# First recurrence of a two-block network: from head pairs one after another to time quarters with all pairs at once

## The chip, the cores and the metric

The kernel runs on one core of a Trainium2 chip. The metric is the device time of one execution in microseconds. It is built as a sequence of blocks of engine programs; between two blocks all engines meet.

## The reference, cut to what matters

The program is two network blocks on 1024 tokens of width 1024. The change is in the first block's recurrence. There are 8 heads of 64 channels; per head a 64x64 state S goes through all tokens:

```
wf = decay_w0 + tanh(wd) @ decay_up;  decay = exp(-exp(-softplus(-wf) - 0.5))
a  = sigmoid(iclr_a0 + ad @ iclr_up);  g = sigmoid(gd) @ gate_up
kk = (k * k_k) normalised per head;    k = k * (1 + (a - 1) * k_a)
S_t = S_{t-1} * decay_t + (S_{t-1} @ -kk_t) (kk_t * a_t)^T + v_t k_t^T
y_t = S_t @ r_t
rwkv_out = (head_group_norm(y) * lnx_g + lnx_b + sum(r * k * r_k) * v) * g
```

Everything is float32. Before this stage a projection has written r, k and v as feature rows, and the low-rank inputs; after it a convolution branch is normalised and both go through an output projection, a feed-forward part, and then the second block.

## The kernel before, in words

All line numbers are those of the profile. `recurrence1` (L513 to L914) holds five engine programs that run beside each other, each in its own order, tied by semaphores. The tokens are cut into 16 chunks of 64. A pair is two heads, one on partitions 0 to 63 and one on 64 to 127. Each engine has one loop over the four pairs, `with pe.Fori(0, PAIRS) as j` on TensorE; the order inside it is written out by hand. Every product is named (`act_names`, `dve_names`, `pe_names`, `pool_names`), the class `Made` counts them on one semaphore per engine, and `need(...)` on TensorE waits for a name. One pass of the loop, for one pair and all its 16 chunks, has these stages:

1. Preparation. TensorE makes the low-rank products `decay` and `iclr` (`broad`, L776, 512 columns each), ScalarE their sigmoids (L639, L641). VectorE scans the logarithms of decay along each chunk (L692) and ScalarE makes three exponentials (L645 to L647). Sums of squares per head go through `stats` (L787), a square root, a reciprocal, a copy to full width and `scales` (L793). VectorE makes the six scaled operands (L709 to L720), each 128x1024.
2. Chunk scores and transposes. `turn` (L825) transposes v, b and k by products with the identity; `LB` and `LK` (L838) are the chunk scores, masked by VectorE (L725).
3. Inverses. For each chunk and head a 64x64 triangular matrix is inverted in 6 levels, in two batches of 8 chunks. GpSimd masks the matrix for a level (L627). TensorE makes T = L X (L782), ScalarE copies it out (L659), TensorE makes two products from it, for X and for its transpose, and VectorE adds them (L739, L740). Level 0 has a product with a unit matrix as well, for the transpose (L734).
4. Chunk walk. For each chunk `ch` in turn: G on TensorE (L874, L875), a copy by ScalarE (L663), U (L782), a copy by VectorE (L743), the state products S (L885, L886), and the new state by VectorE (L748) from those and from the old state scaled by ScalarE (L666). The outputs Y (L892 to L894) are issued after S. All tiles are 64x64 for two heads, and the copies 128x64.
5. Results. Mean, variance, normalisation, the bonus term and the gate (L753 to L768, L776, L787, L793), each 128x1024.

The next pair's stage 1 begins when the results of this one are on their way. The constants (masks) are loaded by the sync engine at the start (L604) and the slices of the low-rank weights in the loop (L611).

Of the kernel before, what the change touches and what calls it, by code (L numbers as in the profile page):

```python
# [14 lines left out]
ALU = mybir.AluOpType  # L15
ACT = mybir.ActivationFunctionType
# [4 lines left out]
P = 128  # L21
T = 1024
# [46 lines left out]
def shape_constants():  # L69
# [15 lines left out]
    out["tile_run"] = np.broadcast_to((np.arange(T2) % P != 0).astype(float), (P, T2))  # L85
    windows = np.array([2, 4, 8, 16])[:, None]
# [422 lines left out]
BATCH = 8  # L509
LEVELS = 6  # L510

def recurrence1(nc, ins, consts, table, ident, rkv, low):  # L513
# [9 lines left out]
    act_names = (["sg", "a", "square", "p", "pinv", "pprev", "kk_std", "v"]  # L523
                 + [f"{x}t{b}" for x in "vbk" for b in range(2)]
                 + [f"T{l}{b}" for l in range(1, LEVELS) for b in range(2)]
                 + [x for ch in range(NC1) for x in ((f"G{ch}", f"SP{ch}") if ch else (f"G{ch}",))]
                 + ["y", "y_square", "y_std"])
    dve_names = ["kkr", "sg_sum", "before_sum", "kk_floor", "kat", "kf", "bon", "kk_inv",
                 "kk_wide"]
    dve_names += ["kk", "at", "rt", "b1", "bt", "kt"]  # L530
    for q in range(4):
        dve_names += [f"LB{q}", f"LK{q}"]
    for b in range(2):
        dve_names += [f"XT0{b}"]
    for b in range(2):
        dve_names += [f"X0{b}"]
    for l in range(1, LEVELS):
        for b in range(2):
            dve_names += ([f"X{l}{b}"] if l < LEVELS - 1 else []) + [f"XT{l}{b}"]
    for ch in range(NC1):  # L540
        dve_names += [f"U{ch}", f"S{ch}"]
    dve_names += ["yc", "y_inv", "y_wide", "yn", "ynorm", "bonus", "ysum", "gated"]
    pe_names = ["decay", "iclr", "kk_stats", "kk_scale"]
    pe_names += ["vt0", "vt1"]
    for q in range(4):
        pe_names += [f"LB{q}", f"LK{q}"]
    pe_names += ["bt0", "bt1", "kt0", "kt1", "T00", "T01"]
    for l in range(1, LEVELS):
        for b in range(2):
            pe_names += [f"T{l}{b}"]  # L550
        for b in range(2):
            pe_names += [f"X{l}{b}"]
    for ch in range(NC1):
        pe_names += [f"G{ch}", f"U{ch}", f"S{ch}", f"Y{ch}"]
    pe_names += ["mean", "y_stats", "y_scale", "bonus", "gate"]
    pool_names = [f"LM{l}{b}" for l in range(LEVELS) for b in range(2)]

    with Scope(nc, "rec1") as s:
        masks = {}
        for name in ("head_ones", "head_sel", "before", "upto", "levels", "eye", "chunk_run"):  # L560
            masks[name] = s.sb(name, [P, CONST_AT[name][1]])
        both = s.sb("both", [P, 2, C1])
        ups = s.sb("ups", [P, 3, P])
        cols = s.sb("cols", [P, 4])
        gn_eps = s.sb("gn_eps", [P, 1])

        def wide(name):
            return s.sb(name, [P, T])

        sg, a, p, pinv, kkr, kk, kf, bon, sq, cumt = map(  # L570
            wide, ("sg", "a", "p", "pinv", "kkr", "kk", "kf", "bon", "sq", "cumt"))
        ar = s.sb("ar", [P, NC1, 2, C1])
        b_, k_, v_ = map(wide, ("b", "k", "v"))
        vt, bt, kt = (s.sb(n, [P, NC1, C1]) for n in ("vt", "bt", "kt"))
        lb, lk = (s.sb(n, [P, NC1, 2, C1]) for n in ("lb", "lk"))
        lm, tt, xx, xt = (s.sb(n, [P, 2, BATCH, C1]) for n in ("lm", "tt", "xx", "xt"))
        floor, std, inv = (s.sb(n, [P, 2 * NT]) for n in ("floor", "std", "inv"))
        gs, us = (s.sb(n, [P, N]) for n in ("gs", "us"))
        st = s.sb("st", [P, 2, N])
        sp_ = s.sb("sp", [P, N])  # L580

        big = s.ps("big", [P, 2, 512])
        big2 = s.ps("big2", [P, 2, 512])
        w = s.ps("w", [P, 4, 512])
        bigf, big2f = (t[:].rearrange("p a b -> p (a b)") for t in (big, big2))
        consts_landed = s.sem("consts_landed")
        ups_landed = s.sem("ups_landed")
        gate_landed = s.sem("gate_landed")
        prepared = s.sem("prepared")
        low_ready = s.sem("low_ready")  # L590
        passed = s.sem("passed")
        cleared = s.sem("cleared")
        A = Made(s.sem("scalar_made"), act_names)
        V = Made(s.sem("vector_made"), dve_names)
        M = Made(s.sem("tensor_made"), pe_names)
        G = Made(s.sem("pool_made"), pool_names)
        block = s.block()
        col = lambda name, j: table[:, bass.ds(j + FIRST[name], 1)]
        heads = [slice(0, N), slice(N, P)]

        @block.sync
        def _(sp):
            for name, tile in masks.items():
                sp.dma_start(tile[:], const_of(consts, name)).then_inc(consts_landed, 16)  # L604
            with sp.Fori(0, PAIRS) as j:
                for n, (name, p0, k, user, landed) in enumerate((
                        ("decay_up", 0, 32, "decay", ups_landed), ("iclr_up", 32, 32, "iclr", ups_landed),
                        ("gate_up", 0, 96, "gate", gate_landed))):
                    M.wait(sp, j, user, back=1)
                    sp.sem_inc(cleared, 1)  # L610
                    sp.dma_start(ups[p0:p0 + k, n, :], ins[name][0, :, bass.ds(j * P, P)]).then_inc(landed, 16)  # L611

        @block.gpsimd
        def _(pool):
            G.start(pool)
            pool.wait_ge(consts_landed, 16 * len(masks))
            with pool.Fori(0, PAIRS) as j:
                for l in range(LEVELS):
                    for b in range(2):
                        if l == 0:  # L620
                            V.wait(pool, j, f"LB{2 * b + 1}")
                        else:
                            M.wait(pool, j, f"T{l - 1}{b}")
                            if l == 1:
                                V.wait(pool, j, f"XT0{b}")
                        mask = masks["levels"][:, l * C1:(l + 1) * C1].unsqueeze(1).broadcast_to((P, BATCH, C1))
                        G.by(nc.gpsimd.tensor_tensor(lm[:, b], lb[:, b * BATCH:(b + 1) * BATCH, 0, :], mask,  # L627
                                                     ALU.mult), f"LM{l}{b}")

        @block.scalar  # L630
        def _(act):
            A.start(act)
            act.wait_ge(consts_landed, 16 * len(masks))
            nc.scalar.activation(low[0:32, 0, :], low[0:32, 0, :], ACT.Tanh).then_inc(low_ready, 1)
            nc.scalar.activation(low[0:96, 1, :], low[0:96, 1, :], ACT.Sigmoid).then_inc(low_ready, 1)
            act.wait_ge(prepared, 4)
            with act.Fori(0, PAIRS) as j:
                M.wait(act, j, "decay")
# [1559 lines left out]
```

## Time and profile before

| | |
|---|---|
| median of 3 runs | 4094.66 us (4094.45 to 4099.09) |
| profiled execution, its own time | 4097.38 us |
| its span, first to last instruction | 4095.4 us |
| TensorE busy over the span | 3402.0 us (83%), 22528 matmul records |
| VectorE, ScalarE, GpSimd busy | 1551.5, 920.9, 865.0 us |
| mean granted TensorE clock | 0.878 of 2.4 GHz |

### The profile page before, as it was taken

The page shows a single profiled execution, that of the slowest core. Times are in us where ns is not written, and L with a number is a line of the kernel's source. Part 1 is how long each engine was busy: PE and PEld are TensorE (multiplying, and loading weights), DVE is VectorE, ACT ScalarE, POOL GpSimd, SP SyncE. Part 2 cuts the span into 40 slices and gives each one's busy share as a digit, 9 for nine tenths or more (in the row PEclk, how much of TensorE's full clock was granted, in tenths as well). Part 3 has the DMA queues.
Part 4 walks back from the last instruction along what each step waited for, and adds up shares of the span by engine and source line. Part 5 has one row for each costly group of instructions (what it writes and reads, how often), then busy time and mean ns, then how long its engine had stood idle before and what let it go on. Part 6 is the DMA issues. An engine that isn't in the chain of part 4 may idle for free. (4 is left out here: it accounts for less than half of the span.)

```text
span 4095.4 us, 55425 instructions
## 1 busy us (share of the span) xinstructions
PE 3402.0 (83%) x22528; PEld 2969.8 (73%) x22528; DVE 1551.5 (38%) x1713; ACT 920.9 (22%) x1209; POOL 865.0 (21%) x404
## 2 busy tenths in 40 slices
PE   5996677776789999997599996666778979999997
PEld 4775576664577777775599995665677668888886
DVE  3894324322323333334200112777753122323334
ACT  2112212213221211212222222333321022121212
POOL 0211011001111211211222212545432012122221
PEclk8997577667799999998699998777778979999998
DMA  2110000002111111111222332000013111111111
GB/s 80 46 32 12 2 2 3 2 2 98 54 44 52 41 51 38 41 43 56 94 93 91 97 89 78 22 31 16 31 49 117 48 52 42 51 41 51 41 51 56
DMA packets 199919, 198.85 MB, mean 49 GB/s; under 512 B 8813, under 2 KB 174661, under 8 KB 199525
## 3 DMA queue, kind: packets, MB, share of 16 engines
q1 hardware_dynamic: 193445, 173.35, 13.2%
q10 hardware_dynamic: 6336, 23.43, 1.6%
q8 instruction: 114, 1.87, 0.2%
q14 instruction: 24, 0.20, 0.0%
HBM read 160.75 MB, written 36.01 MB: 48 GB/s over the span
## 5 line engine op out<-in xcount | busy, mean ns | idle before, releaser
L1202 PE MATMUL ffn_out<-blk_hi,ffn_w_hi 128*128 128x512 f32 (+1 forms) x1584 | 445.1, 372 | 35.4 <-POOL ffn_w_lo L1172 35.4
L1172 POOL TENSOR_TENSOR ffn_w_lo<-ffn_raw,ffn_w_hi 128x1024 fp32r<-128x1024 f32 x88 | 211.5, 2413 | 1186.0 <-ACT ffn_w_hi L1232 1186.0
L1202 PE MATMUL ffn_out<-blk_lo,ffn_w_hi 128*128 128x512 f32 (+1 forms) x1584 | 442.2, 370 | 0.0
L1202 PE MATMUL ffn_out<-blk_hi,ffn_w_lo 128*128 128x512 f32 (+1 forms) x1584 | 441.6, 369 | 0.0
L360 PE MATMUL proj_out<-in_hi,proj_w_hi 128*128 128x348 f32 (+4 forms) x1408 | 335.6, 340 | 24.6 <-POOL proj_w_lo L349 18.9
L1202 PEld LDWEIGHTS ffn_out<-blk_hi,ffn_w_hi 128*128 128x128 f32 x1584 | 291.7, 191 | 79.1 <-POOL ffn_w_lo L1172 19.7
L1216 PE MATMUL ffn_acc<-ffn_d_hi,ffn_hid_hi 128*128 128x512 f32 x704 | 288.0, 409 | 58.9 <-DVE tokens_x L1326 44.2
L360 PE MATMUL proj_out<-in_hi,proj_w_lo 128*128 128x348 f32 (+4 forms) x1408 | 333.5, 338 | 0.0
L360 PE MATMUL proj_out<-in_lo,proj_w_hi 128*128 128x348 f32 (+4 forms) x1408 | 333.3, 338 | 0.0
L1202 PEld LDWEIGHTS ffn_out<-blk_lo,ffn_w_hi 128*128 128x128 f32 x1584 | 290.8, 190 | 43.0
L1202 PEld LDWEIGHTS ffn_out<-blk_hi,ffn_w_lo 128*128 128x128 f32 x1584 | 289.6, 190 | 43.4
L349 POOL TENSOR_TENSOR proj_w_lo<-proj_w_raw,proj_w_hi 128x1024 fp32r<-128x1024 f32 (+1 forms) x66 | 157.5, 2388 | 673.6 <-ACT proj_w_hi L344 673.6
L1216 PE MATMUL ffn_acc<-ffn_d_hi,ffn_hid_lo 128*128 128x512 f32 x704 | 284.5, 404 | 0.0
L1216 PE MATMUL ffn_acc<-ffn_d_lo,ffn_hid_hi 128*128 128x512 f32 x704 | 284.2, 404 | 0.0
L1232 ACT ACTIVATE ffn_w_hi<-ffn_raw 128x1024 fp32r<-128x1024 f32 x88 | 90.7, 1052 | 812.6 <-PE ffn_out L1202 800.5
L360 PEld LDWEIGHTS proj_out<-in_hi,proj_w_hi 128*128 128x128 f32 (+2 forms) x1408 | 242.6, 188 | 42.3 <-POOL proj_w_lo L349 19.4
L1294 DVE SCALAR_TENSOR_TENSOR ffn_y<-ffn_out,top_table,ffn_y 128x1023 f32<-128x1023 f32 x88 | 112.8, 1282 | 381.2 <-ACT ffn_y L1240 375.3
L360 PEld LDWEIGHTS proj_out<-in_lo,proj_w_hi 128*128 128x128 f32 (+2 forms) x1408 | 243.1, 188 | 15.4
L360 PEld LDWEIGHTS proj_out<-in_hi,proj_w_lo 128*128 128x128 f32 (+2 forms) x1408 | 242.9, 188 | 15.3
L1216 PEld LDWEIGHTS ffn_acc<-ffn_d_hi,ffn_hid_hi 128*128 128x128 f32 x704 | 137.2, 195 | 98.9 <-DVE tokens_x L1326 48.5
L484 DVE SCALAR_TENSOR_TENSOR mixed_conv<-mix_c,top_table,mixed_conv 128x1024 f32<-128x1024 f32 x120 | 184.8, 1540 | 3.8
L1326 DVE TENSOR_TENSOR tokens_x<-ffn_acc,tokens_x 128x512 f32<-128x512 f32 x176 | 119.8, 690 | 122.7 <-PE ffn_acc L1216 122.7
(324 smaller groups left out, 5477.7 us busy)
## 6 DMA issues: line engine op xcount, KB each, us to landing
proj<-proj_ev ACTq DMA_DIRECT2D x44, 520.0 KB, 2.7
ffn_raw<-ffn_up SPq DMA_DIRECT2D x44, 512.0 KB, 3.9
proj_w_raw<-w_in SPq DMA_DIRECT2D x44, 512.0 KB, 4.0
ffn_raw<-w_up SPq DMA_DIRECT2D x44, 512.0 KB, 3.9
ffn_d_raw<-ffn_down SPq DMA_DIRECT2D x11, 1024.0 KB, 5.9
ffn_d_raw<-w_down SPq DMA_DIRECT2D x11, 1024.0 KB, 6.0
proj_w_raw<-w_in_first SPq DMA_DIRECT2D x20, 512.0 KB, 4.0
branch_gates<-proj SPq DMA_DIRECT2D x16, 520.0 KB, 4.6
```

Of the source, the lines that this page charges most:

```text
L349: nc.gpsimd.tensor_tensor(self.lo[:, slot, :, 0:m], self.raw[:, slot, :, 0:m], self.hi[:, slot, :, 0:m], ALU.subtract).then_inc(self.lo_re ...
L360: mm = nc.tensor.matmul(out, w[:, slot, k, 0:m], a[:, k, c0:c0 + c], start=k == 0 and part == 0, stop=k == KD - 1 and part == 2)
L484: nc.vector.scalar_tensor_tensor(conv[:, f, :], c[:, f, t:t + T], table[:, column:column + 1], conv[:, f, :], ALU.mult, ALU.add).then_inc( ...
L1172: G.by(nc.gpsimd.tensor_tensor(w_lo[:, i % 2], raw[:, i % 2], w_hi[:, i % 2], ALU.subtract), f"lo{i}")
L1202: mm = nc.tensor.matmul(o, a[:, i % 2, k, :], b[:, k, first:first + n], start=k == 0 and part == 0, stop=k == KD - 1 and part == 2)
L1216: mm = nc.tensor.matmul(acc[:, t % 3, :], a[:, 1 - par, k, i * P:(i + 1) * P], b[:, k, 512 * h:512 * h + 512], start=k == 0 and part == 0, ...
L1232: A.by(nc.scalar.activation(w_hi[:, i % 2], raw[:, i % 2], ACT.Copy), f"hi{i}")
L1294: V.by(vec.scalar_tensor_tensor(y[:, i % 2, back:T], flat[i % 2][:, 0:T - back], column(at, i), y[:, i % 2, back:T], ALU.mult, ALU.add), name)
L1326: V.by(vec.tensor_tensor(dst, acc[:, t % 3, :], dst, ALU.add), f"down{t}")
```

## The change

The loop over pairs becomes a walk over four quarters of the time axis, 4 chunks each, written out without a loop. A quarter's 16 blocks are 4 pairs times 4 chunks, so each elementwise operation still covers 128x1024 or 128x512 elements. The state is a 128x256 tile for all four pairs. In the order of each engine, quarter i's inverses stand among the preparation of quarter i+1 (`more`) and the chunk walk and results of quarter i-1 (`back`). TensorE's new order, from the diff:

```diff
-            with pe.Fori(0, PAIRS) as j:
...
+            for i in range(QUARTERS):
+                more, back = i + 1 < QUARTERS, i > 0
+                if back:
+                    chain_g_keys(0, i - 1)
+                    chain_g_state(0, i - 1)
+                if more:
+                    low_rank("decay", 0, i + 1)
+                    low_rank("iclr", 0, i + 1)
+                if back:
+                    chain_between(0, i - 1)
+                    chain_u(0, i - 1)
...
+                if back:
+                    chain_s(0, i - 1)
+                if more:
+                    key_sum(i + 1)
+                for l in range(1, 4):
+                    level_t(l, 0, i)
+                    if back:
+                        chain_g_state(l, i - 1)
+                    level_t(l, 1, i)
+                    if back:
+                        chain_between(l, i - 1)
+                    level_x(l, 0, i)
+                    if back:
+                        chain_u(l, i - 1)
+                    level_x(l, 1, i)
+                    if back:
+                        chain_s(l, i - 1)
+                    if more and l == 1:
+                        key_spread(i + 1)
+                level_t(4, 0, i)
+                level_t(4, 1, i)
+                if back:
+                    centre(0, i - 1)
...
+                for b in range(2):
+                    scores(f"lbr{b}", range(8 * b, 8 * b + 8), 0, i, slice(1, 2))
+                    level_x(5, b, i)
...
+                for n, (name, b) in enumerate((("vt", 0), ("vt", 1), ("bt", 0), ("bt", 1))):
+                    scores(f"lk{n}", range(4 * n, 4 * n + 4), 1, i, slice(0, 2))
+                    turn(name, b, 2 if name == "vt" else 0, i)
+                if back:
+                    variance(i - 1)
+                for b in range(2):
+                    turn("kt", b, 1, i)
+                for h in range(2):
+                    bonus(h, i)
+                if back:
+                    result_spread(i - 1)
+                    for h in range(2):
+                        low_rank("gate", h, i - 1)
+                if more:
+                    for b in range(2):
+                        removal_scores(b, i + 1)
+            q = QUARTERS - 1
+            chain_g_keys(0, q)
+            for c in range(4):
+                chain_g_state(c, q)
+                chain_between(c, q)
+                chain_u(c, q)
+                chain_s(c, q)
```

Then follow `centre`, `variance`, `result_spread` and the gate of the last quarter. Before the walk stand quarter 0's low-rank products, `key_sum`, `key_spread` and `removal_scores`.

The level products and the walk:

```diff
+            def level_x(l, b, q):
+                pe.wait_ge(tt_ready, 10 * q + 2 * (l - 1) + b + 1)
+                pe.wait_ge(xt_ready, 10 * q + 2 * (l - 1) + b + 1)
+                for i in range(8):
+                    m = 8 * b + i
+                    first, second = (xt, tt) if l < LEVELS - 1 else (tt, xt)
+                    for hd in heads:
+                        last = mm(lv[hd, b, i * C1:(i + 1) * C1], first[hd, m, :], second[hd, m, :], start=True, stop=True,
...
+            def chain_between(c, q):
...
+                for pair, m, hd in each(c):
+                    mm(sn[hd, pair * N:(pair + 1) * N], kt[hd, m, :], vt[hd, m, :], start=pair == 0, stop=False,
...
+                for pair, m, hd in each(c):
+                    out = yp[hd, m // 8, (m % 8) * C1:(m % 8 + 1) * C1]
+                    if n:
+                        mm(out, st[hd, n % 2, pair, :], ar[hd, q % 2, m, 1, :], start=m % 8 == 0, stop=False,
...
+                    mm(out, vt[hd, m, :], lk[hd, m, 1, :], start=n == 0 and m % 8 == 0, stop=False,
...
```

`level_t` is 16 products of 64x64. `chain_g_keys`, `chain_g_state` and `chain_u` are 8 each, `chain_s` 8 for the state, 8 for the outputs and then the next chunk's `chain_g_keys`. On VectorE, the second product of a level is replaced by a transpose in 32x32 squares, and the new state is made by two operations without ScalarE:

```diff
+            def first_level(b, q):
...
+                vec.tensor_tensor(xt[:, blocks(b), :], lm[:, 0, blocks(b), :], eye, ALU.add).then_inc(xt_ready, 1)
+                dve.wait_ge(xt_ready, 10 * q + b + 1)
+                vec.transpose(xx[:, blocks(b), :], xt[:, blocks(b), :]).then_inc(xx_ready, 1)
...
+            def level_turn(l, b, q):
+                dve.wait_ge(xx_ready, 10 * q + 2 * l + b + 1)
+                vec.transpose(xt[:, blocks(b), :], xx[:, blocks(b), :]).then_inc(xt_ready, 1)
...
+            def chain_s(c, q):
...
+                    vec.tensor_tensor(grown[:], new, st[:, n % 2], ALU.add).then_inc(grown_ready, 1)
...
+                vec.tensor_tensor(st[:, (n + 1) % 2], new, decay, ALU.mult).then_inc(st_ready, 1)
```

VectorE's new order; its waits are for the products of the same names:

```diff
+            for i in range(QUARTERS):
...
+                for l in range(1, LEVELS - 1):
+                    level_sum(l, 0, i)
+                    if back and l <= 3:
+                        chain_u(l, i - 1)
+                    level_turn(l, 0, i)
+                    level_sum(l, 1, i)
+                    if back and l <= 3:
+                        chain_s(l, i - 1)
+                    level_turn(l, 1, i)
+                    if more and l == 1:
+                        scan(i + 1)
+                    if more and l == 2:
+                        key_norm(i + 1)
+                        key(i + 1)
+                if more:
+                    decayed(i + 1)
                 for b in range(2):
...
+                    receptance_scores(b, i)
+                    last_level(b, i)
+                if more:
+                    removal(i + 1)
+                key_scores(0, i)
+                if more:
+                    undecayed_key(i + 1)
+                for n in range(1, 4):
+                    key_scores(n, i)
```

Then come `result_inverse`, `bonus`, and of quarter i-1 `normed`, `with_bonus` and `gated`. All products outside the levels and the walk ("pieces") share two PSUM banks `e` in turn, in the fixed order of `quarter_pieces()`; a piece waits until the one before the last has been read out. Sums per head now go through `head_sum` (8 products of 128 columns, all 16 sums of a quarter in 16 rows) and `spread` (8 products of 128 columns). GpSimd makes r times k (`receptance_key`) besides the masks of the levels. The table of constants gets two more masks, `head_window` and `expand` (128x1024); the low-rank weights are loaded once. In `first_block` the tile `c` is freed before the recurrence starts.

## Rows read from the trace of the kernel before

**Rows 1.** Busy time by stretch; with an x, records; then clock, DMA share, GB/s.
```profile
324.20:916.70 592.50, 434.27 (x7472) 381.75 (x7472) 207.76 (x344) 122.09 (x246) 60.52 (x48) 0.70 0.02 4
...
483.10:627.30 144.20, 106.84 (x1868) 94.54 (x1868) 51.19 (x86) 30.02 (x61) 15.13 (x12) 0.72 0.01 3
...
363.00:372.00 9.00, 9.00 (x155) 9.00 (x154) 5.54 (x9) 0.00 (x0) 2.06 (x2) 0.83 0.01 2
372.00:408.60 36.60, 32.76 (x1064) 31.76 (x1059) 14.70 (x22) 8.36 (x14) 13.07 (x11) 1.00 0.02 4
408.60:461.00 52.40, 39.24 (x504) 33.82 (x504) 8.14 (x32) 7.09 (x31) 0.00 (x0) 0.52 0.01 2
461.00:483.10 22.10, 16.89 (x53) 10.34 (x52) 7.78 (x8) 2.35 (x3) 0.00 (x0) 0.68 0.01 4
...
805.25:841.96 36.71, 32.95 (x1066) 31.96 (x1062) 14.78 (x23) 8.36 (x14) 13.16 (x11) 1.00 0.02 4
```
**Rows 2.** Who waited for whom, 324 to 917 us: total, times, longest.
```profile
ACT rec_gs L663 <- PE rec_w L875: 169.5, 60, 3.1
DVE rec_us L743 <- PE rec_w L782: 113.5, 64, 1.9
```
**Rows 3.** Timeline of TensorE, 343 to 380 us: start, duration, instruction group.
```profile
363.86 1.95 PE L838 MATMUL rec_w<-rec_ar,rec_k 64*64 64x128 f32 x16
...
369.35 1.05 PE L838 MATMUL rec_w<-rec_ar,rec_b 64*64 64x128 f32 x16
370.22 1.05 PE L838 MATMUL rec_w<-rec_ar,rec_k 64*64 64x128 f32 x16
...
372.96 2.04 PE L825 MATMUL rec_big<-top_ident,rec_k 64*64 64x64 f32 x64
374.82 2.05 PE L782 MATMUL rec_w<-rec_eye,rec_lm 64*64 64x64 f32 x64
```
**Rows 4.** Timeline of TensorE in the results stage of the last pair.
```profile
906.13 3.75 PE L793 MATMUL rec_big<-top_ident,rec_a 128*128 128x128 f32 x16 [1.47 <-DVE rec_a L757]
...
912.69 1.88 PE L776 MATMUL rec_w<-mix_low,rec_ups 96*128 96x512 f32 x4
```
**Rows 5.** Timeline of TensorE in the chunk walk of the first pair.
```profile
416.36 0.49 PE L885 MATMUL rec_w<-rec_us,rec_bt 64*64 64x64 f32 x4 [0.41 <-DVE rec_us L743]
...
416.60 0.46 PE L886 MATMUL rec_w<-rec_vt,rec_kt 64*64 64x64 f32 x4
```
**Rows 6.** Groups by line on VectorE: busy us, mean ns, idle before and releaser.
```profile
L739 DVE TENSOR_TENSOR rec_xx<-rec_w,rec_xx 128x512 f32<-128x512 f32 x32 | 22.1, 692 | 66.7 <-PE rec_big L782 66.7
...
L743 DVE COPY rec_us<-rec_w 128x64 f32<-128x64 f32 x64 | 14.4, 225 | 113.5 <-PE rec_w L782 113.5
...
L692 DVE TENSOR_TENSOR_SCAN rec_cumt<-rec_chunk_run,rec_sg 128x1024 f32<-128x1024 f32 x4 | 9.2, 2292 | 11.8 <-ACT rec_sg L639 11.8
...
L700 DVE TENSOR_TENSOR rec_kf<-mixed_rkv,rec_kf 128x1024 f32<-128x1024 f32 x4 | 4.9, 1226 | 0.1
```
**Rows 7.** Groups by line on ScalarE and GpSimd, 325 to 920 us.
```profile
L659 ACT ACTIVATE rec_tt<-rec_w 128x512 f32<-128x512 f32 x40 | 23.9, 597 | 99.6 <-PE rec_w L782 99.6
...
L645 ACT ACT_TABLE_LOAD x4 | 5.1, 1283 | 0.1
...
L627 POOL TENSOR_TENSOR rec_lm<-rec_lb,rec_levels 128x512 f32<-128x512 f32 x48 | 60.5, 1268 | 478.3 <-DVE rec_lb L725 415.1 <-PE rec_w L782 63.0
```
**Rows 8.** Timelines of VectorE and GpSimd in the second recurrence.
```profile
2589.52 2.41 DVE L1822 TENSOR_TENSOR rec_z<-rec_q,rec_d 128x520 f32<-128x520 f32 x1
...
2599.64 0.70 DVE L1822 TENSOR_TENSOR rec_z<-rec_k,rec_d 128x520 f32<-128x520 f32 x1
...
2589.00 2.37 POOL L1696 TENSOR_TENSOR rec_d<-rec_a 128x1040 f32<-128x1040 f32 x1
```
**Rows 9.** Timeline at the start of the recurrence.
```profile
324.21 0.34 SPq L604 DMA_DIRECT2D rec_head_ones<-shape_constants  x1
...
331.65 1.05 ACT L634 ACTIVATE mix_low<-mix_low 32x1024 f32<-32x1024 f32 x1 [16.82 <-DMA rec_chunk_run<-shape_constants]
```

More of the change, by code:

```diff
@@ L573, in recurrence1 @@
[L573 to L582, printed above, removed]
@@ L618, in _ @@
+            for i in range(QUARTERS):
                 for l in range(LEVELS):
[L619 to L628, printed above, removed]
+                    mask_level(l, i)
+                if i + 1 < QUARTERS:
+                    receptance_key(i + 1)
@@ new lines, in gated @@
+            def gated(h, q):
+                await_piece(dve, f"gate{h}", q)
+                dve.wait_ge(sum_ready, 2 * q + h + 1)
+                vec.tensor_tensor(rows_of(0, q, h), by_pair(bank(f"gate{h}", q)), by_pair(sqd[:, half(h)]),
+                                  ALU.mult).then_inc(taken(f"gate{h}", q), 1)
+            vec.memset(p[:, :, 0:1], 1.0).then_inc(made, 1)
+            vec.tensor_scalar(keep[:], table[:, FIRST["k_a"]:FIRST["k_a"] + 4], -1.0, 1.0, ALU.mult, ALU.add).then_inc(
+                made, 1)
@@ new lines, in _ @@
+            dve.wait_ge(consts_landed, 16 * len(masks))
+            vec.memset(gn_eps[:], GN_EPS).then_inc(made, 1)
+            vec.scalar_tensor_tensor(center[:], masks["head_ones"][:], -1.0 / N, ident[:], ALU.mult, ALU.add).then_inc(
+                made, 1)
+            vec.tensor_copy(both[:, 0, :], masks["before"][:]).then_inc(made, 1)
+            vec.tensor_copy(both[:, 1, :], masks["upto"][:]).then_inc(made, 1)
+            for pair in range(PAIRS):
+                last = vec.tensor_scalar(rk_ones[:, pair, :], masks["head_ones"][:], col("r_k", pair), None, ALU.mult)
@@ new lines, in start_piece, with end_piece, low_rank @@
+            def start_piece(name, q):
+                b, n = place[name, q]
+                if n > 1:
+                    pe.wait_ge(e_free[b], n - 1)
+                return e[:, b, :]
+            def end_piece(last, name, q):
+                last.then_inc(e_ready[place[name, q][0]], 1)
+            def low_rank(name, h, q):
+                rows, n = {"decay": (slice(0, 32), 0), "iclr": (slice(32, 64), 0), "gate": (slice(0, 96), 1)}[name]
+                out = start_piece(f"{name}{h}", q)
+                for k in range(2):
+                    pair = 2 * h + k
+                    last = mm(out[:, k * QTOK:(k + 1) * QTOK], ups[rows, n, pair * P:(pair + 1) * P],
+                              low[rows, n, toks(q)], start=True, stop=True)
+                end_piece(last, f"{name}{h}", q)
@@ new lines, in bonus, with source @@
+            def bonus(h, q):
+                pe.wait_ge(rkf_ready, q + 1)
+                out = start_piece(f"bon{h}", q)
+                for k in range(2):
+                    pair = 2 * h + k
+                    last = mm(out[:, k * QTOK:(k + 1) * QTOK], rk_ones[:, pair, :], rkf[:, q % 2, pair_cols(pair)],
+                              start=True, stop=True)
+                end_piece(last, f"bon{h}", q)
+            def source(n, m, q):
+                return rkv[:, 4 * n + m // 4, toks(q, m % 4)]
```

861 lines of the change are left out of this document (546 added, 315 removed).

## The prediction, made before the changed kernel was run

> **What bounds the kernel now.** I first laid the page's busy times over the code and found the recurrence by its tiles: its first constant is sent for at 324.2 us and its last operation ends at 916.7, a stretch of 592.5 us [rows 1, 9]. Only this stretch is touched. The busy times by stretch are the next view. A pair takes 144.2 us in the steady state (the two later pairs take the same), TensorE is busy for 107 us of it, VectorE for 51, ScalarE for 30, GpSimd for 15, and the granted clock is 0.72. So TensorE is the engine to look at, and much of its time is slow time. By stage, in the first pair [rows 1]: the inverses (372 to 408.6) run with TensorE busy nine tenths and the clock at 1.00, that is 2.4 GHz. The chunk walk (408.6 to 461) takes 52.4 us for 16 chunks, 3.3 us each, at 0.52, practically the lower level of 1.2 GHz. The results (461 to 483) take 22 us at 0.68, and preparation with scores fills the rest of the pair, some 33 us. The waits show what the walk is [rows 2]: ScalarE waits 60 times for G, up to 3.1 us, VectorE 64 times for U; each engine has one small operation and then waits for the loop to come round. It is a latency loop run 64 times, and nothing stands beside it. Preparation and results are serial in the same way.
>
> **The change part by part.** I count program-level products (two records each), take their pace from the start-to-start distances, and add stalls.
>
> Paces at 2.4 GHz: 32 products of 64x64 start 1.86 us before the next group, 0.058 us each; 8 products of 64x128 take 0.87 us, 0.109 each [rows 3]. At 1.2 GHz, two 64x64 products take 0.24 us, 0.12 each [rows 5]. A 512-column product takes 0.94 us (two in 1.88), so 0.47 for 256 columns. Eight full-size products of 128 columns took 3.75 us right after a wait [rows 4], 0.47 each; I take half of that, 0.235, at full clock.
>
> Work of a middle quarter on TensorE:
> - 64x64: removal and receptance scores 32+32, transposes 96, T 160, X 160, walk 4 chunks of 64, together 736 at 0.058 = 42.7 us. Before, one pair had 252 in the walk, 480 in the levels (the second X product and the level-0 transpose included, 160 more than now).
> - 32 key scores at 0.109 = 3.5.
> - 12 low-rank products of 256 columns at 0.47 = 5.6; 4 for the bonus 1.9; 2 centring products of 512 columns 1.9.
> - 32 products of 128 columns for sums and spreads at 0.235 = 7.5.
> Sum 63 us. Quarter 0 has no walk (14.8), gate, centring, variance or spread of results (7.6): 41. The last has no preparation of a next one (9.5): 54.
>
> What hides what. In levels 1 to 3 of a quarter with a walk, TensorE issues 128 products, 7.5 us. VectorE's share beside it is two sums at 0.69, two transposes, the copy of U and two state operations. The 128x256 operations are not in the trace; between 225 ns for 64 columns and 692 for 512 [rows 6] I take 0.42 us. The 128x512 square transpose isn't there either. Its nearest rows are 692 ns (512 elements) and 1226 ns (1024); I take 0.7 and keep 0.5 and 1.4 as ends, which over 10 transposes a quarter is -2 to +7 us of VectorE work. With 0.7, VectorE has 4.1 us in a level, plus 2.3 for the scan in level 1 [rows 6] or 2.6 for key norm and key in level 2: below 7.5. The copy of G by ScalarE (0.4) runs under the 24 products of `chain_between` (1.4), the copy of U under `level_x(l, 1)` (0.9), the state's two operations (about 1.1 with their hand-offs) under 16 output and key products and `level_t` (1.9). So the walk of three quarters costs its products only. Over a quarter VectorE sums to 43 us, ScalarE (four table loads at 1.28 among it) to about 31, GpSimd to 12 masks at 1.27 and one product of 2.4: 18 [rows 7, 8]. None reaches 63.
>
> Stalls of a middle quarter, from the orders and the two shared PSUM banks. After the last level VectorE has `decayed` (2 x 1.23), the masks of the receptance scores and then `removal` (2 x 1.23) ahead of `key_scores(0)`, while `lk1` waits for `lk0`'s bank: 2.5 us; `undecayed_key` ahead of the next: 0.5. `kt1` waits for ScalarE's table load and root behind `var`: 1. The gate's banks are read only after normalisation, gain, bonus: queued behind them are `lba0` and with it the next quarter's walk: 2.5. Levels 4 and 5 have no walk to fill them: 1.5, and 1 for the rest. Together 9: 72 us for each of two middle quarters, 62 for the last. Quarter 0's levels have no filler. Before, a level with 3.7 us of work for both batches and double X took 6.5; with 3.7 us in all now and a loop through ScalarE and VectorE I take 4.5, so 10 us of stall: 51.
>
> Prologue, from the first constant to the first `level_t`. Constants are ready 7.4 us after the first is sent for [rows 9]; with 512 KB more and three weight loads ahead I take 10.5 (9 to 14). Then small tiles 1, TensorE's `key_sum` at the lower clock 3.8, table and root 1.6, reciprocal 0.5, spread and key norm 4.7, `decayed` 2.5, `removal` 2.5, scores and their copy 2.6, mask 1.4, first level 1.7: 33 us.
>
> Epilogue. The last quarter's walk stands alone: per chunk 64 products, and hand-offs that its own outputs cover only partly. At full clock 4.4 us, at the lower 7.6; the walk before ran at 0.52, which speaks for the latter, the denser work for the former: 4 x 6.3 = 25 (18 to 30). The results of one quarter, in series: two copies, centring, squares, variance, table and root, spread, normalising, gain, bonus, gate: 13 at full, 19 at the lower clock, taken as 16. Before it was 22 for a pair.
>
> Two costs on top. (a) A VectorE operation with two SBUF inputs stops while GpSimd works: the product of 520 elements took 0.70 us alone and 2.41 when it began 0.52 us into a 2.37 us operation of GpSimd, ending 0.56 after it [rows 8]. Two or three such meetings a quarter (a mask against the state's second operation, `receptance_key` against `decayed`) cost 4 us, half of it under TensorE's work: 8 in all. (b) After a wait the first key-score groups took 1.95 us and the later ones 1.05 [rows 3], about 2 us lost each time the clock has to come back: six times, 12 us.
>
> Sum: 33 + 51 + 2 x 72 + 62 + 25 + 16 + 20 = 351 us, say 350, in place of 592.5: 242 less. The profiled execution took 4097.4 (2 around its span), so 3855; the shown median is 2.7 lower, so 3852. The freed tile `c` and what lies behind the recurrence cost nothing.
>
> The Trainium skill, page "SBUF — State Buffer", section "Who interferes with whom", says that the port pair shared by VectorE and GpSimd is an exclusive lock. The trace agrees, as the 0.56 us after GpSimd's end show.
>
> **The rivals.**
>
> *TensorE fully fed.* All stalls are covered and the clock stays up: 33 + 43 + 2 x 63 + 54 + 20 + 14 = 290, so 3792. For it: the inverses run at nine tenths busy. Against: the bank order above.
>
> *Cross-waits.* Four in-order queues with three interleaved jobs: a level and a chunk step then run after each other, 11.5 us instead of 7.5 in three levels, and the quarter's tail stalls 15 to 18 us. Quarters of 92 us: 33 + 58 + 2 x 92 + 82 + 27 + 18 + 10 = 412, so 3914. For it: each hand-off was visible in the walk before, transposes may cost 1.4, and two-input operations meet GpSimd. Against: the slack of 2 to 3 us that VectorE has in each level.
>
> *Lower clock throughout.* The walk had TensorE "busy" three quarters of the time and still ran at 0.52 [rows 1]. If the many short waits keep the clock at 1.2 GHz, a middle quarter has 126 us of products and 9 of stalls: 40 + 90 + 2 x 135 + 115 + 30 + 20 = 565, so 4067. Against: the busy-nine-tenths stretch at 1.00, and the walk's own products fill only about half of its time.
> The page "TensorE: Matmul & The Clock Gate", section "A second HAM failure mode: psum-queue depth-cycling" of the Trainium skill, tells of a kernel that cycled through PSUM banks and whose short pauses made the clock swing. The two banks here are such a case; the stretch of inverses, which goes round banks too, did not swing.
>
> *Slower.* The same lower clock, and stalls of 24 us a quarter instead of 9, because every wait on the two shared banks is then behind a slow product: 40 + 100 + 2 x 150 + 130 + 30 + 20 = 620, so 4122. It decides once the middle quarters pass about 142 us.
>
> Code written out instead of looped is no rival: the first pass through the inverses, new code, ran 1064 matmul records in 36.6 us, and the fourth pass 1066 in 36.7 [rows 1].
>
> **How the numbers follow.** Forecast 0.66 (own range 3815 to 3890), cross-waits 0.20, fully fed 0.07, lower clock 0.05, slower 0.02. The range 3800 to 3935 leaves out the lower clock, the slower case, and the outer parts of cross-waits and of fully fed: under 2 in 10. This kernel can be told from no change by about 0.2%, 8 us. Faster 0.97, same 0.01, slower 0.02.
>
> **What would show it.** The stretch of the recurrence at 330 to 370 us; TensorE's clock above 0.9 from the first level to the last walk; middle quarters (scan to scan) of 68 to 78 us with about 736 small products; the last four chunks 5 to 7 us each; VectorE busy 41 to 50 us a quarter; a transpose of 0.5 to 1.4 us. A quarter above 85 us with the clock up means cross-waits, above 110 with the clock at 0.5 the lower clock. If the later stages change by more than 5 us, something I left out is at work.

## The result, and the profile after

The changed kernel takes 3816.64 us (median; 3814.28 to 3817.67) where the kernel before took 4094.55 (4091.98 to 4099.09) on the same chip: ratio 0.9319 [0.9307, 0.9330], 278 us less. The forecast was 3852 in a range of 3800 to 3935; the gain was 35 us larger than forecast.

The head of the profile's page of the changed kernel: engines' busy time, then the tenths by slice.

```profile
PE 3247.6 (85%) x21568; PEld 2837.7 (74%) x21568; DVE 1509.7 (40%) x1630; ACT 924.1 (24%) x1186; POOL 878.2 (23%) x408
...
PEclk8998998779999999969999978777898799999998
```

The busy times by stretch of the changed kernel, columns as in [rows 1]: prologue, up to the end of the first level operand; quarters 0, 1, 2 and 3, divided where TensorE starts `chain_g_keys(0, ...)`, so that each holds the work that the prediction counts for it; the last walk; the last results; the whole recurrence; all that comes later.

```profile
324.40:354.60 30.20, 16.15 (x120) 12.06 (x120) 15.11 (x26) 15.94 (x29) 4.63 (x3) 0.59 0.19 59
354.60:406.28 51.68, 45.16 (x1073) 41.47 (x1074) 32.78 (x43) 21.74 (x37) 16.72 (x13) 0.90 0.01 3
406.28:475.31 69.03, 64.21 (x1611) 58.88 (x1608) 42.19 (x62) 31.51 (x56) 18.41 (x14) 1.00 0.01 3
475.31:546.34 71.03, 66.47 (x1643) 60.88 (x1641) 40.90 (x63) 31.75 (x56) 18.41 (x14) 0.98 0.01 3
546.34:604.47 58.13, 56.20 (x1532) 52.21 (x1527) 28.59 (x46) 16.96 (x32) 15.39 (x12) 1.00 0.02 4
604.47:624.00 19.53, 16.84 (x513) 15.74 (x512) 6.99 (x15) 2.05 (x6) 0.00 (x0) 1.00 0.02 4
624.00:636.70 12.70, 9.40 (x44) 6.32 (x44) 5.00 (x7) 5.17 (x11) 0.00 (x0) 0.84 0.00 0
324.40:636.70 312.30, 274.42 (x6512) 247.55 (x6512) 171.56 (x261) 125.11 (x223) 73.55 (x52) 0.93 0.03 9
...
636.70:3815.90 3179.20, 2714.06 (x13932) 2381.82 (x13932) 1105.90 (x1196) 735.63 (x888) 752.23 (x330) 0.90 0.17 57
```

The recurrence takes 312.3 us instead of 592.5, with 960 records less (7472 before) and the clock at 0.93 instead of 0.70. The remainder took 3178.7 us before and takes 3179.2 now, so all of the gain is in the stretch that the change touches. TensorE is busy 93% of quarter 1, VectorE 61%.

What one step of the walk is now shows in the timeline of TensorE, ScalarE and VectorE in the last quarter, where it stands alone (start, duration, group): all four pairs in 4.78 us, where one pair took 3.3.

```profile
609.71 0.68 PE L1178 MATMUL rec_gu<-rec_st,rec_ar 64*64 64x64 f32 x16
...
610.44 0.38 ACT L750 ACTIVATE rec_gs<-rec_gu 128x256 f32<-128x256 f32 x1 [4.39 <-PE rec_gu L1178]
...
611.63 0.68 PE L1207 MATMUL rec_gu<-rec_gs,rec_xtf 64*64 64x64 f32 x16
612.35 0.42 DVE L926 COPY rec_us<-rec_gu 128x256 f32<-128x256 f32 x1 [2.69 <-PE rec_gu L1207]
612.83 0.68 PE L1215 MATMUL rec_sn<-rec_us,rec_bt 64*64 64x64 f32 x16 [0.52 <-DVE rec_us L926]
...
614.49 0.68 PE L1178 MATMUL rec_gu<-rec_st,rec_ar 64*64 64x64 f32 x16
```

In a middle quarter the steps disappear between the level products. TensorE at the first level of quarter 1 starts one group after another without a wait:

```profile
416.35 1.15 PE L1136 MATMUL rec_lv<-rec_xx,rec_lm 64*64 64x64 f32 x32
417.33 0.63 PE L1178 MATMUL rec_gu<-rec_st,rec_ar 64*64 64x64 f32 x16
417.80 1.10 PE L1136 MATMUL rec_lv<-rec_xx,rec_lm 64*64 64x64 f32 x32
418.74 0.63 PE L1191 MATMUL rec_sn<-rec_vt,rec_kt 64*64 64x64 f32 x16
```

The waits of the recurrence (total, times, longest) answer to [rows 2]: where ScalarE waited 60 times for G it now waits 7 times, and VectorE, with 64 waits for U before, 7 times as well.

```profile
DVE rec_us L926 <- PE rec_gu L1207: 24.1, 7, 5.7
...
ACT rec_gs L750 <- PE rec_gu L1178: 15.7, 7, 4.4
```

TensorE's own waits between the first level operand and the last walk, 354 to 604 us:

```profile
PE rec_e L1117 <- DVE rec_lk L952: 5.9, 3, 2.0
PE rec_e L1081 <- ACT rec_sg L714: 5.0, 3, 2.6
PE rec_e L1117 <- DVE mixed_rkv L982: 3.0, 2, 1.5
PE rec_lv L1136 <- DVE rec_xx L909: 1.4, 4, 0.9
```

With five smaller ones they come to 17.7 us of 250. The first is `lk1` waiting for its bank, the third `lba0` behind the gate: the two that the prediction named.

### The profile page after: what moved, and what is told of

It reads as the page before. It is cut to its first block and busy times, and to the rows that moved or that the text cites. A ratio compares the mean times of both kernels' runs of the same rounds, so it can differ in the third digit from the quotient of the medians.

```text
span 3815.9 us, 52117 instructions
## 1 busy us (share of the span) xinstructions
PE 3247.6 (85%) x21568; PEld 2837.7 (74%) x21568; DVE 1509.7 (40%) x1630; ACT 924.1 (24%) x1186; POOL 878.2 (23%) x408
## 5 line engine op out<-in xcount | busy, mean ns | idle before, releaser
L364 PEld LDWEIGHTS proj_out<-in_hi,proj_w_hi 128*128 128x128 f32 (+2 forms) x1408 | 242.3, 188 | 42.4 <-POOL proj_w_lo L353 19.5
L488 DVE SCALAR_TENSOR_TENSOR mixed_conv<-in_c,top_table,mixed_conv 128x1024 f32<-128x1024 f32 x120 | 184.8, 1540 | 3.8
```

Of the source, the lines that this page charges most:

```text
L364: mm = nc.tensor.matmul(out, w[:, slot, k, 0:m], a[:, k, c0:c0 + c], start=k == 0 and part == 0, stop=k == KD - 1 and part == 2)
L488: nc.vector.scalar_tensor_tensor(conv[:, f, :], c[:, f, t:t + T], table[:, column:column + 1], conv[:, f, :], ALU.mult, ALU.add).then_inc( ...
```

## The experiments

Every experiment starts from the changed kernel, except the last. Three groups ran, each beside the kernel before: 4089.86 us (4086.12 to 4096.73) in the first, 4096.81 (4091.99 to 4101.11) in the second, 4093.45 (4089.53 to 4098.56) in the third. Groups are compared by ratios. The changed kernel itself ran again in the second; with its ratios of 0.9319 and 0.9324 it stands at 3812.5 us in the first group. The interval of a ratio is about 0.0015 to either side, 6 us, so a difference between two groups isn't known more closely than that; within a group the runs can be compared directly.

### Group 1: where the gain comes from, and what bounds it now

**bunched**: the four steps of the walk stand together ahead of the next quarter's levels, on all engines.

```diff
                 if back:
                     chain_g_keys(0, i - 1)
-                    chain_g_state(0, i - 1)
+                    for c in range(4):
+                        chain_g_state(c, i - 1)
+                        chain_between(c, i - 1)
+                        chain_u(c, i - 1)
+                        chain_s(c, i - 1)
```

> The changed kernel with one thing undone: each quarter's four chunk steps stand together ahead of the next quarter's levels, no longer between them. All pairs still go at once. Theory (the interleaving hides the hand-offs of walk and levels under each other's products): the lone walk after the last quarter takes 4.8 us a chunk, so 19 us, and a level without a chunk step takes 5.2 us in quarter 0, so 3 levels 16; together 35 where levels 1 to 3 and the first chunk step now take 28. Three quarters: +20 us, about 3837. Rival 1 (taking all pairs at once did nearly all of it, the interleaving adds nothing): 3817 to 3822. Rival 2 (the interleaving is the larger part of the 278 us gained): above 3900.

Measured: 3839.86 us (3837.29 to 3843.08), 0.9390 [0.9374, 0.9406], so 27 us more than the changed kernel; 20 were expected. VectorE's copies of U in the walk of quarter 0, columns as above:

```profile
411.73 0.42 DVE L925 COPY rec_us<-rec_gu 128x256 f32<-128x256 f32 x1 [2.88 <-PE rec_gu L1202]
416.51 0.42 DVE L925 COPY rec_us<-rec_gu 128x256 f32<-128x256 f32 x1 [2.69 <-PE rec_gu L1202]
```

They are 4.78 us apart, as in the lone walk. Interleaving is worth 27 us.

**by_pair**: the same, and within a step the four pairs go one after another, with products and copies for one pair (128x64).

```diff
+                for pair in range(PAIRS):
...
+                    last.then_inc(g_ready, 1)
+                    pe.wait_ge(gs_ready, 4 * n + pair + 1)
...
+                    last.then_inc(u_ready, 1)
+                    pe.wait_ge(us_ready, 4 * n + pair + 1)
```

> As the run with the walk bunched, and in the walk the four pairs of a chunk go one after another with 128x64 copies, as in the kernel before (64 latency loops in place of 16). Theory (a step costs hand-offs, whatever its width): a pair's step took 3.3 us before at the lower clock, some 2.9 at the higher; four of them in place of one step of 4.8 us, 16 times, +110 us over the bunched run, +135 if the clock falls: 3945 to 3975. Rival (the batch of pairs only saves small copies): +20 us over the bunched run.

Measured: 3965.13 us (3964.07 to 3970.34), 0.9693 [0.9677, 0.9709], 124 us more than bunched, as expected (110 to 135). VectorE's copies in its last walk:

```profile
641.47 0.22 DVE L930 COPY rec_us<-rec_gu 128x64 f32<-128x64 f32 x1 [1.62 <-PE rec_gu L1251]
644.62 0.22 DVE L930 COPY rec_us<-rec_gu 128x64 f32<-128x64 f32 x1 [1.63 <-PE rec_gu L1251]
```

The latency loop per pair is back, with 3.15 us a step (3.3 in the kernel before), and so is the low clock: 0.50 from 415 to 452 us in its first walk, where bunched has 1.00 in its walk (402 to 424 us). Four steps take 12.6 us where one common step takes 4.78; sixteen times 7.8 is 125. So the 124 us hold two things, fewer hand-offs and the clock that goes with them. before_extra (group 3) puts the low clock at 0.3 to 0.64 us of a pair's step; over 64 steps that is an estimated 20 to 40 of the 124 us.

**twice_t**: every T product of levels 1 to 5 is made twice, 640 products more.

```diff
-                for i in range(8):
+                for i in list(range(8)) * 2:
```

> The changed kernel with every T product of the levels computed twice (640 more products of 64x64, 40 groups of 0.93 us). Theory (TensorE's product time sets the quarters): +37 us less what falls into pauses, 7 in quarter 0 and 1 or 2 elsewhere: +28, about 3845. Rival (hand-offs and VectorE's order set the quarters, TensorE waits for them): under +10.

Measured: 3851.46 us (3847.75 to 3856.74), 0.9420 [0.9404, 0.9436], 39 us more, where 28 were expected: all of 640 x 0.058 = 37 us came through, within the error. The waits of TensorE between level products, which the added ones could fill, had been only 1.6 us. The stretch is bound by TensorE's products.

**twice_turn**: every transpose of levels 1 to 4 is made twice, 32 more on VectorE.

```diff
+                vec.transpose(xt[:, blocks(b), :], xx[:, blocks(b), :]).then_inc(again, 1)
+                dve.wait_ge(again, 8 * q + 2 * (l - 1) + b + 1)
                 vec.transpose(xt[:, blocks(b), :], xx[:, blocks(b), :]).then_inc(xt_ready, 1)
```

> The changed kernel with every transpose of levels 1 to 4 done twice on VectorE (32 more of 0.7 us and a wait each). Theory (VectorE has slack in a level): quarter 0, which has no walk between its levels, pays about 5 us, the others next to nothing: +5 to +8, about 3824. Rival (VectorE's order sets the pace of levels): 32 x 0.8 = +26, about 3843.

Measured: 3822.79 us (3820.25 to 3825.48), 0.9348 [0.9332, 0.9363], 10 us more for 22.8 us of added VectorE time, and 5 to 8 were expected. TensorE's waits for VectorE's sums (L909) grow from 1.4 to 4.8 us, those for the bank of `lk1` from 5.9 to 7.3. VectorE has slack, but not without end.

### Group 2: single stalls

**after_again**: the changed kernel, unedited.

> The changed kernel itself, beside the three variants of this group, so that small differences are read on one chip. Ratio to the kernel before: 0.932.

Measured: 3818.52 us (3817.68 to 3819.71), 0.9324 [0.9311, 0.9337].

**spread_removal**: on VectorE, `removal` of the next quarter is cut in two and stands between the masks of the key scores.

```diff
-                if more:
-                    removal(i + 1)
                 key_scores(0, i)
                 if more:
+                    removal(i + 1, 0)
+                key_scores(1, i)
+                if more:
+                    removal(i + 1, 1)
+                key_scores(2, i)
+                if more:
                     undecayed_key(i + 1)
```

> The changed kernel with VectorE's order at a quarter's end changed: the two operations of removal and undecayed_key stand singly between the four key_scores instead of ahead of the first and second. Theory (TensorE waits 2.0 us for the bank of lk1 while VectorE does removal; in quarter 0 the clock falls after that wait): 3 quarters x 2 us, and 1.5 us for the clock: -6 to -8 us. Rival (the wait only moves, to the later key scores or to the next quarter's removal scores): -2 to +2.

Measured: 3811.66 us (3808.43 to 3813.05), 0.9306 [0.9293, 0.9318], 6.9 us less than after_again, as expected; each of its five runs is faster than each of after_again's. TensorE at that place in quarter 0, first in the changed kernel, then here:

```profile
390.10 1.13 PE L1125 MATMUL rec_e<-top_ident,mixed_rkv 64*64 64x64 f32 x32
393.19 1.44 PE L1117 MATMUL rec_e<-rec_ar,mixed_rkv 64*64 64x128 f32 x16 [1.97 <-DVE rec_lk L952]
394.42 1.93 PE L1125 MATMUL rec_e<-top_ident,mixed_rkv 64*64 64x64 f32 x32
```

```profile
390.76 1.13 PE L1131 MATMUL rec_e<-top_ident,mixed_rkv 64*64 64x64 f32 x32
391.74 1.09 PE L1123 MATMUL rec_e<-rec_ar,mixed_rkv 64*64 64x128 f32 x16
392.67 1.12 PE L1131 MATMUL rec_e<-top_ident,mixed_rkv 64*64 64x64 f32 x32
```

The wait of 1.97 us is gone, and with it the groups behind it that ran at the lower clock (1.93 us for what takes 1.12). In quarter 1 the same wait in the changed kernel is followed by groups of full pace, so this loss of clock doesn't come every time.

**scores_first**: the next quarter's `removal_scores` go ahead of the gate's products, in the bank order and on TensorE.

```diff
-        if back:
-            order += [("gate0", i - 1), ("gate1", i - 1)]
         if more:
             order += [("lba0", i + 1), ("lba1", i + 1)]
+        if back:
+            order += [("gate0", i - 1), ("gate1", i - 1)]
```

> The changed kernel with the next quarter's removal scores ahead of the gate's products in the shared banks. Theory (the removal scores wait for the gate's banks, 1.5 us in quarters 1 and 2, and the masks behind them start late): -3 to -5 us. Rival (the gate's banks are then held longer against the low-rank products of the quarter after, which wait as long): -1 to +2.

Measured: 3812.22 us (3811.14 to 3818.39), 0.9310 [0.9297, 0.9323], 6.3 us less than after_again, where 3 to 5 were expected (one of its five runs, 3818.39, lies among those of after_again). The two waits of `lba0`, 3.0 us, are gone, and two of 0.4 us for ScalarE's copies have come; the rest wasn't traced to a place.

**early_level**: quarter 0's levels start ahead of quarter 1's low-rank products, which then stand between the level products.

```diff
                     if back:
                         chain_g_state(l, i - 1)
+                    elif l <= 2:
+                        low_rank("decay", l - 1, i + 1)
                     level_t(l, 1, i)
```

> The changed kernel with quarter 0's levels started as soon as they can: the preparation products of quarter 1 go between quarter 0's levels instead of ahead of them, with ScalarE's and VectorE's orders moved to match. Theory (the first level's operand is ready at 354.6 us and its product starts at 363.5, behind products that wait for ScalarE's table load; the levels of quarter 0 have 1.5 us of pause each to take them): -6 to -9 us. Rival (later preparation makes quarter 0's end wait for it): -3 to +3.

Measured: 3820.50 us (3818.91 to 3823.92), 0.9331 [0.9318, 0.9344], 2 us more, which is no clear difference; 6 to 9 us less were expected. The theory that the prologue could be shortened this way fell. TensorE there:

```profile
356.94 1.80 PE L1144 MATMUL rec_lv<-rec_xx,rec_lm 64*64 64x64 f32 x32 [3.46 <-POOL rec_lm L666]
358.67 2.07 PE L1089 MATMUL rec_e<-mix_low,rec_ups 32*128 32x256 f32 x4
360.67 1.97 PE L1144 MATMUL rec_lv<-rec_xx,rec_lm 64*64 64x64 f32 x32
```

The levels start 6.6 us earlier but at the lower clock (1.97 us for 32 records instead of 1.15), and the low-rank products that had filled TensorE's time until then have to be made later all the same.

### Group 3: the orders together, and the clock by itself

**two_orders** is spread_removal and scores_first together; **three_orders** has ScalarE's first half of the sigmoids ahead of its squares as well.

```diff
                 if more:
+                    sigmoids(i + 1, [0])
                     squares(i + 1)
-                    sigmoids(i + 1)
+                    sigmoids(i + 1, [1])
```

> The changed kernel with both orders that helped: removal spread between the key scores, and the next quarter's removal scores ahead of the gate. Theory (the two waits are at different places of TensorE's order, so the gains of 6.9 and 6.3 us add): ratio to the kernel before 0.9292, about 3805. Rival (the second wait grows when the first goes, since VectorE then does the same work later): ratio 0.9306, about 3811.

> The same, and ScalarE does the first half of the next quarter's sigmoids before the squares. Theory (the second half's low-rank products wait 1.3 and 1.1 us in quarters 1 and 2, 2.6 in quarter 0, for ScalarE, which does 1.7 us of squares and a table load first; after that wait the clock was low for a few groups in quarter 2): 1.5 to 2 us in each of three quarters: -4 to -6 against the run before, ratio 0.928. Rival (the squares come late now and key_sum waits for them): within 1.5 us of it.

Measured: two_orders 3804.42 us (3803.17 to 3806.28), 0.9294 [0.9281, 0.9307]; three_orders 3801.28 (3799.07 to 3808.0), 0.9290 [0.9278, 0.9303]. By its ratio two_orders is 10 to 12 us faster than the changed kernel (0.9319 and 0.9324), so the two gains of 6.9 and 6.3 us roughly add, as expected. Of the third, TensorE's wait for the sigmoids ahead of quarter 1 shrank from 1.34 to 0.43 us:

```profile
407.54 1.85 PE L1088 MATMUL rec_e<-mix_low,rec_ups 32*128 32x256 f32 x8 [0.43 <-ACT rec_sg L714]
```

But the times overlap, so its worth stays open (3 us by the medians; 4 to 6 were expected). three_orders is the fastest version that ran: 7.1% less time than the kernel before.

**before_extra** is the kernel before with four products of 128 columns added in each step of its walk, which nobody reads.

```diff
                     M.by(last, f"G{ch}")
+                    extra(2)
                     need(A, f"G{ch}")
                     M.by(per_head(w[:, 1, 0:N], x_t, gs), f"U{ch}")
+                    extra(2)
                     need(V, f"U{ch}")
```

> The kernel before with four more products of 128 columns in each step of its chunk walk, two ahead of the wait for ScalarE's copy and two ahead of the wait for VectorE's, written to an unused bank and read by nobody. They ask how much of the old walk (3.3 us a step at a clock of 0.52) was the clock and how much the hand-offs. Theory (hand-offs bound the step; the extra products bring the clock up and fit into the waits): a step falls to 2.7 us, 64 x 0.6 = -38 us, about 4055; so of 210 us of walk only some 40 were the clock. Rival 1 (the clock was the larger part of it): below 4020. Rival 2 (the clock stays low and the extra products lengthen the step by 0.8 us): +50.

Measured: 4071.24 us (4067.13 to 4073.42), 0.9945 [0.9931, 0.9958]: 22 us less than without the added products; 38 less were expected. Its first walk runs at full clock:

```profile
408.60:461.00 52.40, 47.85 (x636) 38.78 (x636) 9.36 (x33) 8.61 (x33) 0.00 (x0) 1.00 0.01 2
```

One step of the kernel before, and one of before_extra, from ScalarE's copy of G on (the last line is VectorE's copy of the next step):

```profile
424.98 0.22 ACT L663 ACTIVATE rec_gs<-rec_w 128x64 f32<-128x64 f32 x1 [2.83 <-PE rec_w L875]
...
425.35 0.48 PE L782 MATMUL rec_w<-rec_gs,rec_xt 64*64 64x64 f32 x4 [0.40 <-ACT rec_gs L663]
425.87 0.23 DVE L743 COPY rec_us<-rec_w 128x64 f32<-128x64 f32 x1 [1.81 <-PE rec_w L782]
426.24 0.49 PE L885 MATMUL rec_w<-rec_us,rec_bt 64*64 64x64 f32 x4 [0.41 <-DVE rec_us L743]
...
429.16 0.23 DVE L743 COPY rec_us<-rec_w 128x64 f32<-128x64 f32 x1 [1.81 <-PE rec_w L782]
```

```profile
426.59 0.22 ACT L663 ACTIVATE rec_gs<-rec_w 128x64 f32<-128x64 f32 x1 [2.50 <-PE rec_w L879]
...
427.13 0.33 PE L782 MATMUL rec_w<-rec_gs,rec_xt 64*64 64x64 f32 x4
...
427.51 0.23 DVE L743 COPY rec_us<-rec_w 128x64 f32<-128x64 f32 x1 [1.55 <-PE rec_w L782]
428.03 0.34 PE L891 MATMUL rec_w<-rec_us,rec_bt 64*64 64x64 f32 x4
...
430.48 0.23 DVE L743 COPY rec_us<-rec_w 128x64 f32<-128x64 f32 x1 [1.57 <-PE rec_w L782]
```

The clock goes from 0.52 to 1.00, and the step from 3.29 us to 2.97. But the added products are in the way themselves. From the start of ScalarE's copy to the product U pass 0.54 us instead of 0.37, from the start of VectorE's copy to S 0.52 instead of 0.37, and TensorE has no wait left at either place. Without these 0.32 us a step at full clock would take an estimated 2.65 us, close to the 2.7 of the theory. So the low clock was a tenth of the old step by the plain difference and about a fifth by this estimate (0.64 us a step, some 41 of 210 us); the remaining four fifths are the chain of products and hand-offs.

## Why the prediction was right, and where it was too careful

**The mechanism held.** The 278 us divide as by_pair 126 (less than before, by its ratio), common steps 124 and interleaving 27. The 124 include the clock that common steps keep up (an estimated 20 to 40 us, see by_pair). The 126 hold together what no run separated: results and preparation beside other work, and 160 level products fewer in each quarter. The latter are 640 products, a number that cost 39 us in twice_t; that the rest comes from the overlap and its higher clock is argued, not shown.

**The terms, one by one.** The prologue has its first level operand (a transpose) at 354.6 us, 30.2 us after the start, for 33 predicted. (The first `level_t`, which the prediction named as its end, starts at 363.5 only, because quarter 1's low-rank products stand ahead of it; the prediction counts their work into quarter 0, and so do the stretches above.) Quarters 0 to 3 take 51.7, 69.0, 71.0 and 58.1 us, for 51, 72, 72 and 62: 249.9 for 257. The last walk takes 19.5 for 25, the last results 12.7 for 16. Then there are 20 us "on top". Together 351 predicted, 312.3 measured.

**What was mis-sized: stalls and the clock.** The largest error is the 20 us on top, for the clock and for the meetings with GpSimd: the quarters came out 7 us under their terms with everything of that kind inside them. The 257 were 221 of products and 36 of stalls. TensorE's waits in the 249.9 are 17.7, which leaves 232 for products at whatever clock: 11 above 221. So 56 us of stalls and allowances were 29. By place:
- Quarter 0 came out at its 51 us, but not by its reason, "levels have no filler", so that is luck. By the starts of the groups its levels 1 to 4 take 4.4 us each for 3.7 us of products, just as predicted (4.5). But 0.8 us in each of five levels is 4 us, not the 10 that the prediction adds. (Its comparison with the kernel before is loose too: a level there had 96 products, 5.6 us, and took 6.7; 3.7 us is the double X alone.) The others went where it named none: 2.9 us of waits for ScalarE's sigmoids and table load ahead of the first level, `lk1` 2.0, and products at the lower clock behind these waits (the stretch has 0.90).
- The middle quarters wait 4.8 and 4.6 us, not 9. `lk1` waits 2.0 (predicted 2.5) and `lba0` 1.5 (2.5); `kt1` and levels 4 and 5 show no wait. Levels 1 to 3 of quarter 1, with a walk between them, take 7.0 to 7.7 us each, where 7.5 were predicted. The sigmoids, 1.3 and 1.1 us, were not named.
- The last quarter waits 1.9 us, for 8 predicted. Two of the named stalls come from the next quarter's `removal` and `removal_scores`, which the last quarter doesn't have; the profile of before and the diff were enough to see that.
- The clock: six losses of 2 us were assumed. The groups that ran slow behind waits at 357, 393 and 480 us took some 5 us longer than the same groups at full pace (an estimate from their starts). The lone walk ran at 1.00, where 25 us had been a mean of both levels: at full clock the prediction's own 4.4 us a step gives 17.6, and 4.78 were measured. The last results ran at 0.84 and took the 12.7 us that the prediction had for full clock (13).
- The meetings with GpSimd, 8 us. They do occur: this `TENSOR_SCALAR` of 128 columns took 1.34 us when it began with a GpSimd mask, and 0.21 in the next quarter.

```profile
364.76 2.50 POOL L666 TENSOR_TENSOR rec_lm<-rec_lba,rec_levels 128x512 f32<-128x512 f32 x2 [4.43 <-PE rec_lv L1136]
...
364.77 1.34 DVE L841 TENSOR_SCALAR rec_std<-rec_std 16x128 f32<-16x128 f32 x1 [7.26 <-ACT rec_std L701]
...
487.78 0.21 DVE L841 TENSOR_SCALAR rec_std<-rec_std 16x128 f32<-16x128 f32 x1 [1.99 <-ACT rec_std L701]
```

What they cost in all show VectorE's groups over the recurrence (busy us, mean ns, idle before and releaser), where an undisturbed L903 takes 0.69 us and an undisturbed L940 0.43:

```profile
L914 DVE STREAM_TRANSPOSE rec_xt<-rec_xx 128x512 f32<-128x512 f32 x32 | 22.6, 707 | 0.5
...
L903 DVE TENSOR_TENSOR rec_xt<-rec_lm,rec_eye 128x512 f32<-128x512 f32 x8 | 7.7, 961 | 3.3 <-POOL rec_lm L666 3.3
L940 DVE TENSOR_TENSOR rec_st<-rec_grown,rec_pend 128x256 f32<-128x256 f32 x15 | 7.5, 500 | 0.5
```

L903 lost 8 x 0.27 = 2.2 us, L940 15 x 0.07 = 1.1, and L841 some 2: about 5 us of VectorE's time, most of which VectorE's slack takes up (twice_turn: 10 us for 22.8). The Trainium skill, page "SBUF — State Buffer", section "Who interferes with whom", speaks of an exclusive lock; the trace agrees with the lock, and its price here was small because few operations met: of these 27, seven took clearly longer.

**The operations bounded from both sides** came out at the chosen values: the transpose 0.707 us (0.7 taken, ends 0.5 and 1.4), the 128x256 operations 0.42 (0.42).

**The rivals.** Cross-waits (3914): the trace has no such quarter; the longest is 71.0 us. Lower clock throughout, and slower: the clock was never at its lower level for a quarter. TensorE fully fed (3792): by number it is 25 us away and the forecast 35, and its last walk and results (20 and 14) were the nearer ones. By mechanism it is not it either: its quarters sum to 223 us, the measured ones to 249.9, and the bank waits that the forecast named were there and paid when taken out (two_orders, 10 to 12 us). But it had deserved more than 0.07.

**What was to show it.** Missed: the stretch was to be 330 to 370 us, and is 312; the last four steps were to take 5 to 7 us each, and take 4.8; VectorE was to be busy 41 to 50 us a quarter, and is in quarter 1 (42.2) and all but in quarter 2 (40.9), not in 0 and 3 (32.8, 28.6), which have less work. Met: the clock (0.99 from the first level product to the last walk), the middle quarters (69.0 and 71.0 us, and 71.0 from the scan in quarter 1 to that in quarter 2, for 68 to 78, with 806 and 822 products of all kinds where the prediction counts 818), the transpose (0.707 us, the 0.7 taken), and the later stages (0.5 us off).

## What to carry to other kernels

In this kernel, where a step is a chain of small hand-offs, putting independent recurrences into one step (4 pairs in 4.78 us instead of 3.3 each) was worth 124 us, its higher clock included, and putting other work between the hand-offs 27 more. To predict such an interleaving, sum the busiest engine's work at full pace and add only the waits that can be named from the queue and bank orders of that very stage; don't carry a middle stage's stalls over to the last, and don't add general allowances on top: here they were the largest error. And when added work is used as a probe, as in before_extra, look whether it delays the chain itself before reading the difference of the times.

## What was not expected of the hardware

- A RECIPROCAL on 16x128 took 0.94 us, on 128x16 in the kernel before 0.25. Both have 2048 elements, so the shape with more columns was the slower one, and it is much longer than a TENSOR_SCALAR of the same 16x128 (0.21).
- Four added products per step, which nobody reads, made the kernel before 22 us faster: they raised the clock from 0.52 to 1.00 and cost less than that gave back (before_extra).
- A wait of 1.97 us was followed by groups at the lower clock in quarter 0 and by none in quarter 1.
